# Hybrid diffusion step on one core: expert tiles renumbered, an add wait removed, adaLN sums in the eighth bank, last down product by halves

## The chip, the cores and the metric

One core of one Trainium2 chip. The metric is the device time of one execution in microseconds; of several runs the median is given. Everything is fp32.

## The reference, cut to what matters

Two trunk layers over 640 tokens (512 latent tokens and 128 context tokens, 1024 columns). Layer 0 mixes tokens by latent attention with 16 heads, layer 1 by neighbourhood attention. After each comes a mixture of experts: 16 experts in 4 groups of 4; a token picks one group and two experts in it. Each sub-layer has adaLN: shift, scale and gate rows computed from a conditioning vector by one product with a 1024 x 6144 matrix per layer.

```python
_, top_group = lax.top_k(group_score, TOPK_GROUPS)          # TOPK_GROUPS = 1
expert_mask = jnp.repeat(group_mask, EXPERTS_PER_GROUP, axis=-1) > 0
_, top_e = lax.top_k(jnp.where(expert_mask, biased, NEG_INF), TOP_K)   # TOP_K = 2
...
act = jax.nn.silu(jnp.einsum('td,edf->tef', t, w_gate)) * jnp.einsum('td,edf->tef', t, w_up)
act = act * gates.astype(act.dtype)[..., None]
return jnp.einsum('tef,efd->td', act, w_down).reshape(shp)
```

So the two experts of a token are always of one group, and two experts of different groups share no token.

## The kernel before, in words

Each engine has its own hand-written program, and semaphores join them. The program of one engine is strictly in order; a wait holds everything behind it on that engine. GpSimd (POOL) issues the gathers, the adds and the small stores; SyncE (SP) issues the weight loads; ScalarE (ACT) issues the loads and stores of x and h. The PSUM has eight banks of 512 columns.

**Attention of layer 0** (`mla_scores`, `mla_between`, `mla_pT`, `mla_pv`, L1036 to L1110). It runs over 40 steps w, five token tiles for each of eight head pairs. In step w TensorE makes the scores of the pair's two heads (L1065, L1068; banks 0 and 1, banks 2 and 3), then the transposes of step w-1 (banks 4 and 5, banks 6 and 7, at most 384 columns of each), then the product with V of step w-2. In one step of each pair an adaLN product (`ada(0, 4 + p)`, L809, 64 matmuls of 128 columns) stands between the two heads' scores. Its sums go to bank 3, columns 128 to 255 (`ada_bank`, `ada_out_at`), where the second head's scores come next. So TensorE waits for `m_cp` before them: VectorE's `ada_rows` has added the bias to the sums and written them to `modrow` (two operations for two of the eight). The adaLN product itself waits for `a_ex`, the exponentials of step w-1.

**Experts.** `f_stage` chooses experts and builds, on VectorE, tables of the tokens and gates of each tile of 128 slots; `tables_out` (L1955) copies them out of PSUM. Tile n holds the first 128 tokens of expert `EXPERT[n]`; slots without a token name a spare row behind the 640 real rows of the buffers in HBM. There are 15 static tiles (STAT), then the last expert's tile and the overflow tiles in a loop of 1 to 5 passes with two tiles each; `rtx` holds the count of passes and the experts. For a tile, POOL gathers the token rows, TensorE transposes them (`rows_T`), multiplies by gate and up weights (`gateup`, L1194), transposes the activations (`acts_T`), multiplies by the down weights (`down`, L1211), VectorE scales the result to `yb[n % 2]` (`y_out`), and POOL adds the rows to x in HBM with an accumulating indirect DMA (`add_rows`, L734; `add_static`). The tables are stored by expert number, and tiles of odd n use a second table (`odd_at`) with other spare rows.

Adds go through two semaphores `e_ys[l][0]` and `[1]`, 16 for each add, by the parity of the tile. Fourteen static adds leave both at 112. In a pass of the loop POOL issues a gather, waits in mid-pass until both counters are at 112 (128 in the second pass, and so on), issues a second gather, and then the two adds:

```python
for j in range(2):
    pool.wait_ge(e_yd[l], i * 2 + (STAT + j))
    pool.wait_ge(e_ys[l][1 - j], i * 16 + (112, 128)[j])
    pool.nop().then_inc(e_gate, 1)
    add_rows(last_token(j), j)
```

**The last tile** isn't added in HBM. Its down product goes to banks 1 and 2, VectorE writes y, and TensorE multiplies y by a 0/1 matrix (`at_token`) that puts its rows in token order (`last_part`, L1253), two products for each of five tiles of x. Meanwhile ACT waits for both add counters, in layer 0 also for the adaLN product `ada(1, 4)` (its weights lie in x's place), and loads the five tiles of x (L1628). VectorE's `x_sum` (L1698 on `resid`) adds the two. In layer 0 `ada(1, 4)` stands behind the last down product and ahead of `last_part`. After that come layer 1's norm, its transposes and the value projection (L934), or in layer 1 the final norm and the stores.

Of the kernel before, what the change touches and what calls it, by code (L numbers as in the profile page):

```python
# [57 lines left out]
EXPERT = (0, 4, 12, 8, 1, 5, 13, 9, 2, 6, 11, 7, 3, 10, 14)  # L58
ODD = slice(4, 11)
# [7 lines left out]
C_SPARE, C_SPARE_ODD = 257, 258  # L67
# [15 lines left out]
def constants():  # L83
    c = np.zeros((P, NCONST + NK), np.float32)
    p = np.arange(P)
    c[:, C_ID:C_ID + P] = np.eye(P)
    c[:, C_TRI:C_TRI + P] = p[:, None] < p[None, :]
    c[:, C_ONE:C_ONE + P] = 1.0

    qc, kc = p // ROWS, np.arange(LOCAL) // ROWS  # L90
    for n, (q0, k0) in enumerate(((0, 0), (48, 32))):
        q, k = q0 + qc[:, None], k0 + kc[None, :]
        start = np.clip(q - 8, 0, GRID_W - 16)
        at = C_MASK + n * LOCAL
# [8 lines left out]
    c[:, C_I16:C_I16 + E] = np.arange(E)  # L103
# [7 lines left out]
    c[:, C_SPARE] = TOK + p - 2048  # L111
    c[:, C_SPARE_ODD] = TOK + P + p - 2048
# [4 lines left out]
    k[:, K_BASE:K_BASE + E] = P * (E - 1) - np.arange(E) * P  # L117
    k[:, K_FIRST:K_FIRST + E] = E - np.arange(E)
    return c


def build(nc, a, o):

    with ExitStack() as ctx:
# [22 lines left out]
        rtx = sb("tiles", 32, 1, I32)  # L147
        wrt = sb("wrouter", KD * E)
        info = sb("info", 37)
# [76 lines left out]
        tok_at, gate_at, odd_at = info[:, 0:STAT], info[:, STAT:2 * STAT], info[:, 2 * STAT:2 * STAT + 7]  # L226
# [28 lines left out]
        hD, xD = ([nc.dram_tensor(f"{n}rows{l}", [TOK + spares * P, D], F32).ap() for l in range(DEPTH)] for n, spares in (("h", 1), ("x", 2)))  # L255
# [316 lines left out]
        def _(pool):  # L572
# [136 lines left out]
            for l in range(DEPTH):  # L709
# [21 lines left out]
                rows_of(tok_at[:, EXPERT[2]:EXPERT[2] + 1], 0)  # L731
# [8 lines left out]
                def add_static(n):  # L740

                    pool.wait_ge(e_yd[l], n + 1)
                    at, e = (odd_at, EXPERT[n] - ODD.start) if n % 2 else (tok_at, EXPERT[n])
                    add_rows(at[:, e:e + 1], n % 2)

                for n in range(3, STAT + 2):
# [3 lines left out]
                    rows_of(tok_at[:, EXPERT[n]:EXPERT[n] + 1] if n < STAT else last_token(n - STAT + 3), n % 2)  # L750
# [8 lines left out]
                with pool.Fori(0, trips) as i:  # L759
                    pool.wait_ge(e_tr[l], i * 2 + (STAT + 1))  # L760
# [24 lines left out]
        def _(pe):  # L785
# [262 lines left out]
            def mla_scores(w):  # L1048
# [6 lines left out]
                for par in range(2):  # L1055
# [5 lines left out]
                    if par and i == (1 if p else 0):  # L1061
                        pe.wait_ge(m_cp, 5 + p)
# [114 lines left out]
            def moe(l):  # L1177
# [25 lines left out]
                def down(b, w_in_, w_ready, tiles, free):  # L1203
# [8 lines left out]
                    ins.then_inc(e_dn[l], 1)  # L1212
# [21 lines left out]
                down(2, e_dw[l][0], trips * 16 + 16, trips * 2 + STAT, trips * 2 + (STAT - 1))  # L1234
                pe.wait_ge(e_dn[l], trips * 2 + STAT)

                pe.wait_ge(e_ta[l], trips * 2 + (STAT + 1))
                pe.wait_ge(e_td[l], trips * 2 + (STAT + 1))
                if l == 0:
                    ada(1, 4)  # L1240
                pe.wait_ge(e_yd[l], trips * 2 + STAT)
                pe.wait_ge(e_sel, l + 1)
                for t in range(4):
                    last_part(l, t)

            def last_part(l, t):
# [5 lines left out]
                for n in range(2):  # L1252
                    ins = pe.matmul(part_at(l, t)[:, n * 512:(n + 1) * 512], at_token[:, t * P:(t + 1) * P], yb[0][:, n * 512:(n + 1) * 512],  # L1253
# [14 lines left out]
            for u, (t, j) in enumerate(WIN):  # L1268
# [9 lines left out]
                if u == 0:  # L1278
                    last_part(0, 4)
# [97 lines left out]
            last_part(1, 4)  # L1377
# [3 lines left out]
        def _(act):  # L1381
# [153 lines left out]
            act.wait_ge(s_yz, 16 * 6)  # L1535
# [153 lines left out]
        def _(dve):  # L1689
# [85 lines left out]
            for b in (3, 6, 7):  # L1775
                link(dve.memset(bank(b, P, P if b == 3 else 0), 0.0))
# [103 lines left out]
            dve.wait_ge(s_yz, 16 * 6)  # L1880
# [74 lines left out]
            def tables_out(l):  # L1955

                dve.wait_ge(rr_cnt, 8 * l + 8)
                spare = const[:, C_SPARE:C_SPARE + 1]
# [3 lines left out]
                dve.tensor_scalar(odd_at.bitcast(U32), toks[:, ODD], const[:, C_SPARE_ODD:C_SPARE_ODD + 1], 2048.0, ALU.min, ALU.add)  # L1962
                for at in (last_tok[:, 2:15], last[:, 0]):
                    dve.tensor_scalar(at.bitcast(U32), toks[:, STAT - 1:], spare, 2048.0, ALU.min, ALU.add)
                dve.tensor_copy(last[:, 1], gates[:, STAT - 1:]).then_inc(e_tab[l], 1)

            def f_stage(l):
# [18 lines left out]
                tx, cmp_, at = rt[0:1, 1100:1132], rt[0:1, 1140:1284], rt[:, 1290:1310]  # L1986
# [79 lines left out]
                def first_places(t):  # L2066

                    dve.wait_ge(rr_cnt, 8 * l + max(t + 1, 2))
                    link(dve.scalar_tensor_tensor(out=u2[:, t], in0=rank[:, t, EXPERT[0]:EXPERT[1] + 1:EXPERT[1]], scalar=1.0, in1=M[:, t, EXPERT[0]:EXPERT[1] + 1:EXPERT[1]], op0=ALU.add, op1=ALU.mult))
# [61 lines left out]
                link(tt(pos, pos, const[:, C_E128:C_E128 + E].unsqueeze(1).to_broadcast([P, NT, E]), ALU.add))  # L2131
# [20 lines left out]
                link(dve.tensor_copy(tx[:, MAXT:MAXT + 5], const[0:1, C_FREE:C_FREE + 5]))  # L2152
                cm = cmp_.rearrange("p (x e) -> p x e", x=XTILES)
# [9 lines left out]
            def moe(l):  # L2163
# [38 lines left out]
                for n in range(STAT):  # L2202
                    if n == 2:
                        dve.wait_ge(e_tab[l], 1)
                    acts(gate_at[:, EXPERT[n]:EXPERT[n] + 1], n + 1, n or None)
# [4 lines left out]
                    if n < STAT - 1:  # L2210
                        gate_rows(tok_at[:, EXPERT[n]:EXPERT[n] + 1], 3 * n + 1, 3 * n + 2)
# [24 lines left out]
                y_out(trips * 2 + STAT, trips * 8 + (base + 3), 0, trips * 16 + 16 * 7)  # L2236
# [130 lines left out]
```

## Time and profile before

| | |
|---|---|
| runs, median of 3 | 1307.62 us (1306.54 to 1309.13) |
| the profiled execution's own time | 1304.3 us |
| its span | 1302.4 us, 19449 instructions |
| mean granted TensorE clock | 0.99 |
| TensorE matmuls busy | 1239.2 us, 95% |
| VectorE, ScalarE, GpSimd busy | 653.0, 341.8, 221.1 us |
| HBM traffic over the span | 203 GB/s |

In the timeline a row has its start in us from the span's start, the length in us of the row, the engine, the line, the operation, and what it writes and reads. "x64" says that 64 instructions of one kind are merged, and brackets give how long the engine sat idle before it and what released it. L1698 is a helper for VectorE's `tensor_tensor`, so the tile's name says which use it is. A row of windows has the stretch, then for each engine its busy time and instructions, the granted clock of TensorE as a part of full speed, the share of the DMA engines and GB/s. The span is slightly shorter than the time, and the profiled execution is 3.3 us below the median.

### The profile page before, as it was taken

The numbers are of one execution on the slowest core, as the hardware profiler recorded it, in microseconds if no ns is written. First come the engines' busy times: TensorE is split into PE (matmuls) and PEld (weight loads), VectorE is DVE, ScalarE is ACT, GpSimd is POOL, SyncE is SP. The second block draws the span as 40 slices with busy tenths as digits, with TensorE's granted clock in tenths as the row PEclk, the third lists the DMA queues.
The fourth block names the chain that finished last, engine by engine and source line by source line (L and its number), as shares of the span: only waits on it lengthen the run. The fifth ranks groups of instructions, "written<-read, shape, count | busy, mean of one in ns | idle before, by whom it ended". The sixth has DMA issues, their size and how long they took to land.

```text
span 1302.4 us, 19449 instructions
## 1 busy us (share of the span) xinstructions
PE 1239.2 (95%) x7503; PEld 713.0 (55%) x7503; DVE 653.0 (50%) x1612; ACT 341.8 (26%) x797; POOL 221.1 (17%) x298
## 2 busy tenths in 40 slices
PE   5899999999999999999989999999999998999995
PEld 3665466666645554444444455556884455444442
DVE  5221266556626664444455335432883666444446
ACT  4121255445403400000032000103891340000002
POOL 6220500010010012222120001040321001222220
PEclk8999999999999999999999999999999999999998
DMA  9612411131475459999971274542316336999966
GB/s 383 226 41 75 182 70 67 67 131 67 196 265 195 162 202 380 379 380 378 347 228 79 74 257 171 194 145 79 87 51 254 140 130 260 374 379 380 379 173 202
DMA packets 45450, 267.83 MB, mean 206 GB/s; under 512 B 6980, under 2 KB 13460, under 8 KB 31520
## 3 DMA queue, kind: packets, MB, share of 16 engines
q1 hardware_dynamic: 22672, 192.85, 37.9%
q0 software_dynamic: 16928, 52.77, 14.4%
q10 hardware_dynamic: 5760, 20.97, 4.2%
q8 instruction: 60, 0.98, 0.3%
q14 instruction: 30, 0.25, 0.1%
HBM read 230.19 MB, written 34.81 MB: 203 GB/s over the span
## 4 chain that ended last, share of the span: by engine, by line
PE 86%; DVE 6%; DMA 4%; issue 2%; ACT 1%; POOL 0%; ACTq 0%; POOLq 0%; DVEq 0%
PE PS L1194 15%; PE PS L934 13%; PE PS L1299 11%; PE PS L1148 10%; PE PS L1211 8%; PE PS L787 5%; PE PS L1065 5%; PE PS L793 4%; PE PS L1105 3%; PE PS L1357 2%; PE PS L809 2%; PE PS L1015 2%; PE PS L1320 1%; DVE big L1698 1%; PE PS L1068 1%
## 5 line engine op out<-in xcount | busy, mean ns | idle before, releaser
L1148 PE MATMUL PS<-weights,ht 128*128 128x512 f32 x320 | 142.4, 596 | 1.0 <-DVE ht L1698 1.0
L1299 PE MATMUL PS<-ht,weights 128*128 128x128 f32 (+1 forms) x512 | 140.2, 435 | 0.8 <-DMA weights<-in_qkv 0.8
L934 PE MATMUL PS<-weights,ht 128*128 128x336 f32 (+1 forms) x320 | 115.8, 520 | 1.6 <-ACT ht L1480 1.6
L1194 PE MATMUL PS<-big 128*128 128x512 f32 x256 | 113.1, 594 | 0.5 <-DVE big L2166 0.5
L1299 PEld LDWEIGHTS PS<-ht,weights 128*128 128x128 f32 x512 | 77.8, 191 | 63.4 <-issue 62.3
L787 PEld LDWEIGHTS PS<-const,big 128*128 128x128 f32 (+2 forms) x627 | 77.0, 144 | 57.1 <-issue 39.9
L787 PE MATMUL PS<-const,big 128*128 128x128 f32 (+2 forms) x627 | 92.1, 283 | 12.4 <-DVE big L1788 4.2
L1608 ACT ACTIVATE big<-PS 128x256 f32<-128x256 f32 x34 | 13.0, 383 | 337.1 <-PE PS L1194 337.1
L1148 PEld LDWEIGHTS PS<-weights,ht 128*128 128x128 f32 x320 | 59.0, 190 | 68.2 <-issue 68.2
L934 PEld LDWEIGHTS PS<-weights,ht 128*128 128x128 f32 x320 | 60.1, 190 | 52.2 <-issue 38.1
L1194 PE MATMUL PS<-weights,big 128*128 128x512 f32 x192 | 84.4, 592 | 0.0
L1698 DVE TENSOR_TENSOR big<-PS,big 128x512 f32<-128x512 f32 (+1 forms) x70 | 44.2, 672 | 69.8 <-PE PS L1211 69.8
L1194 PEld LDWEIGHTS PS<-big 128*128 128x128 f32 x256 | 47.4, 190 | 54.5 <-issue 54.5
L1942 DVE TENSOR_REDUCE stats<-PS 128x1 f32<-128x640 f32 (+1 forms) x80 | 56.7, 716 | 40.2 <-PE PS L1068 36.8
L611 POOL DMA_DIRECT2D modrows<-modrow x32 | 18.4, 583 | 342.6 <-DVE modrow L1698 263.3
L1698 DVE TENSOR_TENSOR big<-big,PS 128x256 f32<-128x256 f32 x34 | 14.3, 420 | 121.0 <-ACT big L1608 121.0
L1065 PE MATMUL PS<-big 96*128 96x512 f32 x128 | 69.2, 623 | 4.2 <-DVE modrow L1698 2.5
L1562 ACT ACTIVATE rows<-PS,stats 128x640 f32<-128x640 f32 (+1 forms) x80 | 56.4, 705 | 49.6 <-issue 32.5
L1211 PE MATMUL PS<-rows,big 128*128 128x512 f32 x144 | 65.1, 595 | 1.4 <-DVE big L2180 1.2
L1758 DVE SCALAR_TENSOR_TENSOR rows<-weights,condT,rows 128x512 f32<-128x512 f32 x98 | 65.5, 745 | 0.0
L734 POOL DMA_INDIRECT xrows<-big,info x28 | 44.4, 1586 | 117.4 <-DVE big L1698 117.4
L934 PE MATMUL PS<-weights,rows 128*128 128x384 f32 (+1 forms) x168 | 60.5, 518 | 0.2 <-ACT big L1519 0.2
(256 smaller groups left out, 1837.0 us busy)
## 6 DMA issues: line engine op xcount, KB each, us to landing
weights<-in_ada SPq DMA_DIRECT2D x22, 2048.0 KB, 8.9
big<-in_gu SPq DMA_DIRECT2D x16, 2048.0 KB, 20.1
weights<-in_gu SPq DMA_DIRECT2D x12, 2048.0 KB, 23.6
rows<-in_down SPq DMA_DIRECT2D x18, 1024.0 KB, 14.3
weights<-in_down SPq DMA_DIRECT2D x16, 1024.0 KB, 17.3
ht<-in_gu SPq DMA_DIRECT2D x6, 2048.0 KB, 23.0
weights<-in_qkv SPq DMA_DIRECT2D x6, 2048.0 KB, 8.6
weights<-in_wo SPq DMA_DIRECT2D x4, 2048.0 KB, 7.9
```

The lines of the kernel that those rows point to most:

```text
L787: return pe.transpose(dst, src, const[0:n, C_ID:C_ID + n])
L793: ins = pe.transpose(dst[:, at + 512 * r:at + 512 * r + 64], src[rows], const[rows, C_ID + 64 * r:C_ID + 64 * r + 64])
L934: ins = pe.matmul(bank(4 + u % 2, n), lhs(k), rhs(k), start=(k == 0), stop=(k == ks - 1))
L1065: pe.matmul(bank(2 * par), lhs, kTh[h % 4][0:QD, 0:512], start=True, stop=True)
L1148: ins = pe.matmul(bank(4 + j), OT[:, k, t * P:(t + 1) * P], w[j][:, k, :], start=(k == 0), stop=(k == KD - 1))
L1194: ins = pe.matmul(bank(0), gatT[:, k, :], w[:, k, :], start=(k == 0), stop=(k == KD - 1))
L1211: ins = pe.matmul(bank(1 + n), actT[:, k, :], w[:, k, n * 512:(n + 1) * 512], start=(k == 0), stop=(k == 1))
L1299: ins = pe.matmul(bank(bb, n1 - n0), w[:, k, m * P:(m + 1) * P], hT[:, k, n0:n1], start=(k == 0), stop=(k == KD - 1))
L1562: act.activation(dst, src, ACT.Exp, scale=sign, bias=st[:, 100 + at:101 + at], accum_out=st[:, 104 + at:105 + at]).then_inc(a_ex, 1)
L1698: return dve.tensor_tensor(dst, x, y, op)
L1758: dve.scalar_tensor_tensor(out=acc[c], in0=w[:, k, :], scalar=by, in1=acc[c], op0=ALU.mult, op1=ALU.add).then_inc(m_acc, 1)
L1942: dve.tensor_reduce(st[:, at:at + 1], bank(2 * par, n), AXX, ALU.max, negate=True).then_inc(a_mx, 1)
```

## The change

The parts of the diff:

1. `EXPERT` becomes 0, 4, 8, 12, 1, 5, 9, 13, 2, ... (groups in turn), and the tables are laid out by tile number instead of expert number. Even and odd tiles get their spare rows by a step of two over one table; `odd_at` goes. `hD` has two spare blocks as `xD` has. `tables_out` has eight operations, before it had six.
2. In the loop POOL waits for values that are read from a table (`C_LANDED`: 96, 128, 144, 160, 176) by a register load.
3. The adaLN sums of products 4 to 11 go to bank 7, columns 384 to 511. The wait for `m_cp` moves from before the second head's scores to before the second head's transposes, and the product waits for `a_pd`, VectorE's copy of the transposes of step w-2.
4. `ada(1, 4)` moves ahead of the last down product. That product signals after each half of its columns, VectorE writes y by halves and signals each, and `last_part` begins with the first.

```diff
-EXPERT = (0, 4, 12, 8, 1, 5, 13, 9, 2, 6, 11, 7, 3, 10, 14)
-ODD = slice(4, 11)
+EXPERT = [4 * (n % 4) + n // 4 for n in range(E)]
...
+    c[:, C_LANDED:C_LANDED + 5] = [96, 128, 144, 160, 176]
...
         def ada_bank(i):
-            return 2 if 12 <= i < 16 else 3 if 4 <= i < 12 else 6 + i % 2
+            return 2 if 12 <= i < 16 else 7 if 4 <= i < 12 else 6 + i % 2
         def ada_out_at(i):
-            return ada_bank(i) * 512 + (128 if 4 <= i < 12 else 0)
+            return ada_bank(i) * 512 + (384 if 4 <= i < 12 else 0)
...
             for l in range(DEPTH):
-                pool.dma_start(hD[l][TOK:, :], zero).then_inc(s_yz, 16)
-                for n in range(2):
-                    pool.dma_start(xD[l][TOK + n * P:TOK + (n + 1) * P, :], zero).then_inc(s_yz, 16)
+                for r in range(2):
+                    rows = slice(TOK + r * P, TOK + (r + 1) * P)
+                    pool.dma_start(hD[l][rows, :], zero).then_inc(s_yz, 16)
+                    pool.dma_start(xD[l][rows, :], zero).then_inc(s_yz, 16)
...
                 with pool.Fori(0, trips) as i:
+                    landed = pool.value_load(rtx[0:1, bass.ds(i + 32, 1)], min_val=96, max_val=176)
...
-                        pool.wait_ge(e_ys[l][1 - j], i * 16 + (112, 128)[j])
+                        pool.wait_ge(e_ys[l][1 - j], landed + (0, 16)[j])
...
                     if w:
-                        pe.wait_ge(a_ex, 2 * w)
+                        pe.wait_ge(a_pd, w - 1)
                     ada(0, 4 + p)
...
-                    if par and i == (1 if p else 0):
-                        pe.wait_ge(m_cp, 5 + p)
...
                     at = (4 + 2 * par) * 512
+                    if par and w % NT == 0:
+                        pe.wait_ge(m_cp, 5 + w // NT)
...
-                    ins.then_inc(e_dn[l], 1)
+                        if n or by_halves:
+                            ins.then_inc(e_dn[l], 1)
...
-                down(2, e_dw[l][0], trips * 16 + 16, trips * 2 + STAT, trips * 2 + (STAT - 1))
-                pe.wait_ge(e_dn[l], trips * 2 + STAT)
-
+                if l == 0:
+                    ada(1, 4)
+                down(2, e_dw[l][0], trips * 16 + 16, trips * 2 + STAT, trips * 2 + (STAT - 1), True)
...
-                if l == 0:
-                    ada(1, 4)
...
-                dve.tensor_scalar(tok_at.bitcast(U32), toks[:, 0:STAT], spare, 2048.0, ALU.min, ALU.add).then_inc(rr_info, 1)
+                for r in range(2):
+                    spare = const[:, C_SPARE + r:C_SPARE + r + 1]
+                    ins = dve.tensor_scalar(tok_at[:, r::2].bitcast(U32), toks[:, r:STAT:2], spare, 2048.0, ALU.min, ALU.add)
+                ins.then_inc(rr_info, 1)
...
-                y_out(trips * 2 + STAT, trips * 8 + (base + 3), 0, trips * 16 + 16 * 7)
+                dve.wait_ge(e_gr[l], trips * 8 + (base + 3))
+                dve.wait_ge(e_ys[l][0], trips * 16 + 16 * 7)
+                for n in range(2):
+                    half = slice(n * 512, (n + 1) * 512)
+                    dve.wait_ge(e_dn[l], trips * 2 + (STAT + n))
+                    tt(yb[0][:, half], bank(1 + n), grow[:, half], ALU.mult).then_inc(e_yd[l], 1)
```

## Rows read from the trace of the kernel before

**Rows 1.** The page, chain that ended last, shares of the span by engine.

```profile
PE 86%; DVE 6%; DMA 4%; issue 2%; ACT 1%; POOL 0%; ACTq 0%; POOLq 0%; DVEq 0%
```

**Rows 2.** Line L1065, TensorE's idle time before it: releaser, us, times.

```profile
  DVE modrow L1698: 2.5, 5
  DVE modrow L1771: 1.7, 2
```

**Rows 3.** Timeline, first attention: the first and the second head pair.

```profile
156.71 0.49 PE L1070 MATMUL PS<-big 96*128 96x128 f32 x2 [0.41 <-DVE modrow L1698]
...
178.32 0.96 DVE L1920 COPY rows<-PS 128x768 f32<-128x768 f32 x1 [0.45 <-PE PS L793]
...
180.88 1.93 PE L809 MATMUL PS<-weights,condT 128*2 128x128 f32 x64
...
182.87 0.29 DVE L1698 TENSOR_TENSOR modrow<-PS,ada_bias 128x128 f32<-128x128 f32 x1 [1.06 <-PE PS L809]
...
183.31 1.10 PE L1065 MATMUL PS<-big 96*128 96x512 f32 x2 [0.51 <-DVE modrow L1698]
```

**Rows 4.** Timeline, the table step of layer 0.

```profile
474.06 0.23 DVE L1960 TENSOR_SCALAR info<-PS,const 128x15 uint32<-128x15 f32 x1 [0.52 <-PE PS L903]
...
474.55 0.36 DVE L1964 TENSOR_SCALAR big<-PS,const 128x13 uint32<-128x13 f32 x2
...
474.90 0.41 DVE L1698 TENSOR_TENSOR big<-big,PS 128x256 f32<-128x256 f32 x1
...
476.58 7.11 PE L1194 MATMUL PS<-big 128*128 128x512 f32 x16 [0.25 <-DVE big L2166]
```

**Rows 5.** Timeline, GpSimd behind its zero stores, and ScalarE's first q store.

```profile
48.02 0.54 POOL L635 DMA_DIRECT2D big<-in_krope  x1
...
89.41 0.49 ACT L1519 ACTIVATE big<-PS 128x384 f32<-128x384 f32 x1
```

**Rows 6.** Timeline, end of layer 0's expert stage.

```profile
652.99 1.61 POOL L734 DMA_INDIRECT xrows<-big  x1 [0.30 <-issue]
...
653.43 1.29 DVE L1698 TENSOR_TENSOR big<-PS,big 128x512 f32<-128x512 f32 x2 [1.78 <-PE PS L1211]
...
660.87 3.70 PE L1211 MATMUL PS<-rows,big 128*128 128x512 f32 x8 [0.60 <-DVE big L2180]
660.92 1.58 POOL L734 DMA_INDIRECT xrows<-big  x1 [6.32 <-DMA xrows<-big]
...
664.91 1.93 PE L809 MATMUL PS<-resid,condT 128*2 128x128 f32 x64 [0.35 <-PE PS L1211]
666.77 7.13 PE L1253 MATMUL PS<-big 128*128 128x512 f32 x16
...
667.11 2.73 ACTq L1628 DMA_DIRECT2D resid<-xrows  x5
...
673.88 1.22 DVE L1698 TENSOR_TENSOR resid<-resid,PS 128x1024 f32<-128x1024 f32 x1 [1.91 <-DMA resid<-xrows]
```

**Rows 7.** Transfers into or out of xrows, 600 to 672; and a window's row.

```profile
DMA to landing us min/median/max: 3.5/7.4/13.5
...
676.00:677.00 1.00, 0.98 (x5) 0.98 (x6) 1.00 (x1) 0.58 (x3) 0.00 (x0) 0.56 0.98 307
```

**Rows 8.** Timeline, end of layer 1's expert stage.

```profile
1269.94 1.29 DVE L1698 TENSOR_TENSOR big<-PS,big 128x512 f32<-128x512 f32 x2 [1.78 <-PE PS L1211]
...
1275.20 1.58 POOL L734 DMA_INDIRECT xrows<-big  x1 [6.84 <-DMA xrows<-big]
...
1281.29 1.29 DVE L1698 TENSOR_TENSOR big<-PS,big 128x512 f32<-128x512 f32 x2 [0.21 <-PE PS L1211]
...
1282.83 8.82 PE L1253 MATMUL PS<-big 128*128 128x512 f32 x20 [1.76 <-DVE big L1698]
1284.92 1.22 DVE L1698 TENSOR_TENSOR resid<-resid,PS 128x1024 f32<-128x1024 f32 x1 [2.34 <-DMA resid<-xrows]
...
1286.54 1.22 DVE L1698 TENSOR_TENSOR resid<-resid,PS 128x1024 f32<-128x1024 f32 x1 [0.40 <-PE PS L1253]
```

More of the change, by code:

```diff
@@ L66 @@
 C_MASK = 384
-C_SPARE, C_SPARE_ODD = 257, 258
+C_SPARE = 257
+C_T128, C_LANDED = 260, 280
 C_COS, C_SIN = 896, 960
@@ L110, in constants @@
     c[:, C_SEL:C_SEL + E] = p[:, None] % 32 == np.arange(E)[None, :]
-    c[:, C_SPARE] = TOK + p - 2048
-    c[:, C_SPARE_ODD] = TOK + P + p - 2048
+    for r in range(2):
+        c[:, C_SPARE + r] = TOK + r * P + p - 2048
+    first_tile = np.argsort(EXPERT) * P
+    c[:, C_T128:C_T128 + E] = first_tile
+    c[:, C_LANDED:C_LANDED + 5] = [96, 128, 144, 160, 176]
     k = c[:, NCONST:]
@@ L146, in build @@
         rti = sb("slot_of", 6 * NT, P, U32)
-        rtx = sb("tiles", 32, 1, I32)
+        rtx = sb("tiles", 40, 1, I32)
         wrt = sb("wrouter", KD * E)
-        info = sb("info", 37)
+        info = sb("info", 30)
         rbias = rt[:, 1420:1436]
@@ L254, in build @@
         toepD = nc.dram_tensor("toeplitz", [H, 2 * ROWS, TLEN], F32).ap()
-        hD, xD = ([nc.dram_tensor(f"{n}rows{l}", [TOK + spares * P, D], F32).ap() for l in range(DEPTH)] for n, spares in (("h", 1), ("x", 2)))
+        hD, xD = ([nc.dram_tensor(f"{n}rows{l}", [TOK + 2 * P, D], F32).ap() for l in range(DEPTH)] for n in "hx")
         s_const, s_x, s_vec, s_par, s_ck = (sem(n) for n in ("const_in", "x_in", "vec_in", "gains_and_router_in", "mlacache_in"))
@@ L742, in add_static @@
                     pool.wait_ge(e_yd[l], n + 1)
-                    at, e = (odd_at, EXPERT[n] - ODD.start) if n % 2 else (tok_at, EXPERT[n])
-                    add_rows(at[:, e:e + 1], n % 2)
+                    add_rows(tok_at[:, n:n + 1], n % 2)
                 for n in range(3, STAT + 2):
@@ L749, in _ @@
                     pool.wait_ge(e_tr[l], n - 1)
-                    rows_of(tok_at[:, EXPERT[n]:EXPERT[n] + 1] if n < STAT else last_token(n - STAT + 3), n % 2)
+                    rows_of(tok_at[:, n:n + 1] if n < STAT else last_token(n - STAT + 3), n % 2)
                     if n >= 4:
@@ L1201, in acts_T, with down @@
                     ins.then_inc(e_at[l], 1)
-                def down(b, w_in_, w_ready, tiles, free):
+                def down(b, w_in_, w_ready, tiles, free, by_halves=False):
                     pe.wait_ge(w_in_, w_ready)
@@ L1252, in last_part @@
                 for n in range(2):
+                    if n and t == 0:
+                        second_half()
                     ins = pe.matmul(part_at(l, t)[:, n * 512:(n + 1) * 512], at_token[:, t * P:(t + 1) * P], yb[0][:, n * 512:(n + 1) * 512],
@@ L1376, in _ @@
             moe(1)
-            last_part(1, 4)
+            last_part(1, 4, None)
         @block.scalar
@@ L1534, in _ @@
             cq_out(3)
-            act.wait_ge(s_yz, 16 * 6)
+            act.wait_ge(s_yz, 16 * 8)
             q_store(0)
@@ L1772, in ada_rows @@
                 ins.then_inc(m_cp, 1)
-            for b in (3, 6, 7):
-                link(dve.memset(bank(b, P, P if b == 3 else 0), 0.0))
+            for b, at in ((6, 0), (7, 0), (7, 384)):
+                link(dve.memset(bank(b, P, at), 0.0))
             dve.wait_ge(s_vt, 1)
@@ L1879, in _ @@
             ckv_out(3)
-            dve.wait_ge(s_yz, 16 * 6)
+            dve.wait_ge(s_yz, 16 * 8)
             q_store(1)
@@ L1957, in tables_out @@
                 dve.wait_ge(rr_cnt, 8 * l + 8)
-                spare = const[:, C_SPARE:C_SPARE + 1]
                 toks, gates = bank(6, TILES), bank(6, TILES, TILES)
-                dve.tensor_scalar(tok_at.bitcast(U32), toks[:, 0:STAT], spare, 2048.0, ALU.min, ALU.add).then_inc(rr_info, 1)
+                for r in range(2):
+                    spare = const[:, C_SPARE + r:C_SPARE + r + 1]
+                    ins = dve.tensor_scalar(tok_at[:, r::2].bitcast(U32), toks[:, r:STAT:2], spare, 2048.0, ALU.min, ALU.add)
+                ins.then_inc(rr_info, 1)
                 link(dve.tensor_copy(gate_at, gates[:, 0:STAT]))
-                dve.tensor_scalar(odd_at.bitcast(U32), toks[:, ODD], const[:, C_SPARE_ODD:C_SPARE_ODD + 1], 2048.0, ALU.min, ALU.add)
                 for at in (last_tok[:, 2:15], last[:, 0]):
-                    dve.tensor_scalar(at.bitcast(U32), toks[:, STAT - 1:], spare, 2048.0, ALU.min, ALU.add)
+                    for r in range(2):
+                        spare = const[:, C_SPARE + r:C_SPARE + r + 1]
+                        dve.tensor_scalar(at[:, r::2].bitcast(U32), toks[:, STAT - 1 + r::2], spare, 2048.0, ALU.min, ALU.add)
                 dve.tensor_copy(last[:, 1], gates[:, STAT - 1:]).then_inc(e_tab[l], 1)
@@ L2068, in first_places @@
                     dve.wait_ge(rr_cnt, 8 * l + max(t + 1, 2))
-                    link(dve.scalar_tensor_tensor(out=u2[:, t], in0=rank[:, t, EXPERT[0]:EXPERT[1] + 1:EXPERT[1]], scalar=1.0, in1=M[:, t, EXPERT[0]:EXPERT[1] + 1:EXPERT[1]], op0=ALU.add, op1=ALU.mult))
+                    link(dve.scalar_tensor_tensor(out=u2[:, t], in0=rank[:, t, 0:EXPERT[1] + 1:EXPERT[1]], scalar=1.0, in1=M[:, t, 0:EXPERT[1] + 1:EXPERT[1]], op0=ALU.add, op1=ALU.mult))
                     dve.tensor_scalar(hot[0][:, t, :], rk[:, K_IOTA:K_IOTA + P], u2[:, t, 0:1], None, ALU.is_equal).then_inc(rr_hot, 1)
@@ L2130, in f_stage @@
                 link(tt(pos, pos, rank, ALU.add))
-                link(tt(pos, pos, const[:, C_E128:C_E128 + E].unsqueeze(1).to_broadcast([P, NT, E]), ALU.add))
+                link(tt(pos, pos, const[:, C_T128:C_T128 + E].unsqueeze(1).to_broadcast([P, NT, E]), ALU.add))
                 for c in range(2):
```

21 lines of the change are left out of this document (11 added, 10 removed).

## The prediction, made before the changed kernel ran

> **What bounds the kernel now.** I read the page first, then the chain that ended last, then the timeline where that chain leaves TensorE. The chain is 86% TensorE [rows 1], so an edit pays only where it takes something out of TensorE's line, or out of one of the short stretches where the chain leaves it. The change touches four such stretches: the eight head pairs of the first attention, the table step before each expert stage, the end of the first expert stage, and the end of the second.
>
> **First attention.** TensorE makes the two score products of a step, and in one step of each head pair it puts an adaLN product (L809, 64 matmuls, 1.93 us) between them. That product went to bank 3, which the second score product also writes, so TensorE then waited until VectorE had copied it out: 0.51 us in the pass shown [rows 3]. Over the stage these waits come to 2.5 us in five passes and 1.7 in two where VectorE makes two operations [rows 2], and 0.41 in the first pass [rows 3]: 4.6 in all. With the sums in bank 7 the second score product can follow at once. The wait moves ahead of the second head's transposes, which write bank 7. The score products between take over 1.1 us (their first part alone is 1.10), while the copy ended 0.35 us after the adaLN product (182.81 to 183.16), in the two longer passes some 0.3 later: both are over before the new wait. The adaLN product itself now waits for VectorE's copy of step w-2 out of banks 6 and 7. In the shown pass that copy ended at 179.28, 1.6 us before the product began [rows 3]: no cost. What follows on TensorE ran without a gap, so ScalarE and VectorE don't end it. I take 4.4 of the 4.6, since the gap left between two products isn't quite nothing, with 3.9 and 4.6 as ends.
>
> **Table step, twice.** It has 8 VectorE operations in place of 6: one more before the first gather is released, one more behind it. It is on the path: the second gate-up product waits for VectorE behind it [rows 4]. Three such operations took 474.55 to 474.90, 0.12 us each; the first, whose end something waits for, lasts 0.23. Two more cost 0.25 in a layer, 0.5 in both, with 0.4 and 0.9 as ends. The gather that is released some 0.15 later is wanted a whole gate-up product later, at 7 us: covered. The extra copy into the row of tile numbers falls into TensorE's table product, where VectorE sat idle 0.52 us [rows 4]: nothing; without that cover, 0.2.
>
> **Zero rows.** Two more stores of 512 KB from GpSimd, and everything behind them on its queue a microsecond later. The queue had issued all six and the krope load by 48.6; the first consumer, ScalarE's q store, ran at 89.41 [rows 5]. With 40 us of cover this is nothing, and nothing else of GpSimd's is due before.
>
> **End of the first expert stage.** Here the chain leaves TensorE. There is one pass of the dynamic loop in this trace, with the adds of tiles 14 and 15. GpSimd issued the first at 652.99, then sat 6.32 us until it had landed, and issued the second at 660.92, though its rows were ready at 654.72 (653.43 + 1.29) [rows 6]. ScalarE started the five loads of x at 667.11 when that landed, 6.2 us after its issue; VectorE's second x sum waited for them, 1.91 us, to 673.88 [rows 6]. Of the two waits that now use the new register only the second changes: both counters must reach 112 in mid-pass anyway, so the first never held anything. With it gone the second add follows the first. GpSimd has one more register load ahead of its gather; the trace times none, only the 0.30 before the first add in which the queue handles a wait, an increment and the issue; I take 0.5, with nothing and 1.0 as ends. That puts the first add at 653.5 and, after its 1.61 us and a gap of 0.3, the second at 655.4. How long it takes to land beside another is what the trace shows least: alone 6.2 us, the first one, beside a gather, until 660.9, up to 7.9; across the stage 3.5 to 13.5 with 7.4 as the median [rows 6, 7]. I take 7.4, nearest to the pair with a gather: landed at 662.8.
>
> Two other things must be ready then. ScalarE also waits for the adaLN product that reads its weights out of x. It moves ahead of the last down product: TensorE came free at 660.27 (0.60 before 660.87), so its 1.93 run to 662.2 and the down product starts at 662.25 instead of 660.87. The loads can go at 662.8, 4.3 us sooner. The token-order products (L1253, 7.13 us for four tiles) began at 666.77. Now the down product ends at 662.25 + 3.70 = 665.95; the first half of y, 0.65 us of VectorE after the down product's first half (664.1), is there by then, the second at 666.8, and the products start at 666.0 and go on without a gap, since the first takes 0.89 (7.13 / 8). Their second tile is done at 669.6, and that is as soon as the second x sum can run: 673.88 less 669.6 is 4.3, the same as the loads give. I take 3.8, since TensorE ends its four tiles only at 673.1 and must make the transposes after that; ends 1.0 (landing at 666) and 4.4. Further on, the projection, its weight loads (they wait for x loads and for TensorE itself) and the bias loads all shift along. The Trainium skill, "DMA: Bandwidth & Descriptors", section "Anatomy of one DMA", fits a GpSimd DMA as 2.0 us plus its bytes at 436 GB/s, an estimated 3.2 us for 512 KB; the lone add's row says 6.2 and decides. By the page the adaLN product would be the last to end and this term would be 4.4 in place of 3.8.
>
> **End of the second expert stage.** No adaLN product here. The second add was issued at 1275.20, and with the 6.2 us of the lone add x was loaded from about 1281.4; VectorE waited 2.34 us for it, to 1284.92; the second sum waited 0.40 for TensorE, to 1286.54 [rows 8]. Two edits meet. The second add goes 3.9 us sooner (its rows are ready at 1269.94 + 1.29), so x isn't last any more. And y comes by halves: VectorE had to make the selection matrix until 1281.1 and made y at 1281.29 to 1282.58; the products began at 1282.83 after a wait of 1.76 [rows 8]. Its first half can now run from 1281.1, so the products start at 1281.9, and while the first one runs (0.89 us) the second half comes. That is 0.9 us. From the second sum on the stage goes at VectorE's pace and keeps the shift. I take 0.9; ends 0.3 (x still late) and 1.2.
>
> **Renumbering** changes no count and no size: the same experts' weights, 15 static tiles, one pass. It lets neighbours be in flight, and costs nothing elsewhere.
>
> **Sum.** -4.4 + 0.5 - 3.8 - 0.9 = -8.6 us. The profiled execution took 1304.3 us, which becomes 1295.7; it lay 3.3 under the median of the runs, 1307.62, and the same sum against that is 1299.0.
>
> **Rivals.** (a) The two adds share the DMA engines and come out one behind the other: the second lands at 665 to 666, the first stage's end brings 1.5, and the sum is 6.3: 1301.3. For it: the first add took up to 7.9 beside a gather, the queue's median is 7.4 with weight loads beside, and GpSimd's adds read and write HBM [rows 6, 7]. Against it: at 655 to 663 the weight loads have mostly landed. The Trainium skill, same page, section "Issuing engines are not separate DMA queues", says that all DMAs run on the same 16 engines and interleave; so it speaks for this rival, and this trace has no two adds in flight to say by how much.
> (b) The attention's stalls come back elsewhere: VectorE's copy, the maxima and the next head's keys are late in turn, and 4.4 goes. The sum is 4.2: 1303.4. Against it, TensorE had no other gap in these passes, and the 1.28 us of score products cover a copy of 0.35.
> (c) The change doesn't do what it says: the loop's second wait still holds, because the add of tile 13 or the mid-pass wait on both counters is what ends last. Then only the attention and y by halves are left: 4.4 + 0.3 - 0.5 = 4.2, again 1303.4.
> (d) Slower. Both adds, the gather and, in the first layer, what is left of the loads slow each other so that the second add lands L us after its issue, and x is late by L - 11.7 in the first layer (655.4 against 667.1) and by L - 10.1 in the second (1271.3 against 1281.4). Against 4.4 saved and 0.5 paid, this passes +2.6 us from L = 14.2; with L = 15 it is 3.3 + 4.9 + 0.5 - 4.4 = +4.3, 1311.9. For it: 13.5 was seen for one transfer of this stage [rows 7]. Against it: that was beside weight loads.
> Something smaller goes either way. TensorE's granted clock averaged 0.56 from 676 to 677, so it was at 1.2 GHz for most of that, after the engine had been idle from 673.9 (666.77 + 7.13) [rows 6, 7]. In the new order that idle time is nearly gone, so the clock may stay at 2.4 GHz; VectorE's part is as long as before, so this is worth 0 to 0.5.
>
> **How the numbers follow.** A measurement of this kernel can tell some 0.2%, 2.6 us, from no change. Chances: my forecast 0.70, (a) 0.14, (b) and (c) 0.10 together, (d) 0.02; 0.04 for what I haven't seen, most of it within 0.2%. The forecast's own ends are -8.6 with 3.9, 4.4, 1.2, 0.3 and their opposites; all at once isn't likely, so 1297.2 to 1301.0. The range reaches through (a) to (b) and (c): 1296.6 to 1303.5. Faster by over 0.2% holds in all cases but (d), the unseen, and a small part of (b) and (c) where more is lost: 0.93; same 0.04, slower 0.03.
>
> **What would show it.** Right: no wait of L1065's products for modrow; the adaLN product and the second score product back to back; two GpSimd adds some 2 us apart in both layers; ScalarE's x loads near 662.8 on the old time scale; the first value projection 3.8 us sooner after the last gate-up; the last stage's products on y starting 0.9 sooner. Wrong: a new wait of the second head's transposes or of L809; x loads that still follow the second add by more than 9 us; a time over 1303.5.

## The result, and the profile after

The changed kernel took 1295.14 us (median of 6 runs, 1292.16 to 1300.87), the kernel before 1307.08 on the same chip: a ratio of 0.9912, with a 95% interval of 0.9889 to 0.9935. That is faster, as forecast, but by 11.5 us by the ratio (11.9 between the medians) where 8.6 were forecast, and 1.5 us below the range. Two more series of the changed kernel gave 0.9916 and 0.9922, so the best figure is about 10.9 us. The profiled execution took 1296.04 us, its span was 1294.3.

The chain that ended last is now 90% TensorE, from 86 [rows 1]; the page's row:

```profile
PE 90%; DVE 5%; ACT 2%; DMA 1%; issue 1%; ACTq 0%; DVEq 0%; SPq 0%
```

The first attention after, by the idle time ahead of TensorE's first score product (the answer to [rows 2]) and by the timeline of the second head pair (to [rows 3]; a row has start, length, engine, line, operation):

```profile
L1067 PE MATMUL PS<-big x128: 591/594/697, 158.0 to 346.9; 96*128 96x512 f32 x128
its engine sat idle before it (us, times) until:
  issue: 7.0, 30
  ACT rows L1567: 1.4, 8
```

```profile
179.25 0.96 DVE L1925 COPY rows<-PS 128x768 f32<-128x768 f32 x1 [0.45 <-PE PS L797]
...
181.81 1.93 PE L813 MATMUL PS<-weights,condT 128*2 128x128 f32 x64
...
183.67 1.13 PE L1067 MATMUL PS<-big 96*128 96x512 f32 x2
...
183.81 0.29 DVE L1703 TENSOR_TENSOR modrow<-PS,ada_bias 128x128 f32<-128x128 f32 x1 [1.06 <-PE PS L813]
```

No wait for modrow is left (the two idle times in the first fence are those of the weight loads, which run beside the products), and the score product starts as the adaLN product ends. The end of the first expert stage after, from its timeline (to [rows 6]):

```profile
650.58 1.61 POOL L738 DMA_INDIRECT xrows<-big  x1 [0.30 <-issue]
652.49 1.58 POOL L738 DMA_INDIRECT xrows<-big  x1 [0.30 <-issue]
```

```profile
656.80 1.93 PE L813 MATMUL PS<-resid,condT 128*2 128x128 f32 x64
...
658.66 3.70 PE L1215 MATMUL PS<-rows,big 128*128 128x512 f32 x8
...
660.24 2.43 ACTq L1633 DMA_DIRECT2D resid<-xrows  x5
...
662.20 6.36 PE L1258 MATMUL PS<-big 128*128 128x512 f32 x14
...
666.02 1.22 DVE L1703 TENSOR_TENSOR resid<-resid,PS 128x1024 f32<-128x1024 f32 x1 [0.49 <-PE PS L1258]
```

```profile
669.26 1.99 PE L791 MATMUL PS<-const,big 128*128 128x128 f32 x16
671.96 7.11 PE L938 MATMUL PS<-weights,ht 128*128 128x512 f32 x16 [0.71 <-ACT ht L1654]
```

The three fences are GpSimd's own rows, all engines' rows, and TensorE's own rows behind them. The adds go 1.9 us apart, the loads of x (L1633) 7.75 us after the second, and the second x sum waits for TensorE and no longer for a load. The end of the second stage (to [rows 8]):

```profile
1265.00 1.58 POOL L738 DMA_INDIRECT xrows<-big  x1 [3.76 <-DVE big L1703]
...
1273.04 2.27 ACTq L1633 DMA_DIRECT2D resid<-xrows  x5
...
1273.88 1.28 DVE L1703 TENSOR_TENSOR big<-PS,big 128x512 f32<-128x512 f32 x2
1274.82 8.82 PE L1258 MATMUL PS<-big 128*128 128x512 f32 x20 [0.86 <-DVE big L1703]
1276.81 1.22 DVE L1703 TENSOR_TENSOR resid<-resid,PS 128x1024 f32<-128x1024 f32 x1 [1.65 <-PE PS L1258]
...
1278.53 1.22 DVE L1703 TENSOR_TENSOR resid<-resid,PS 128x1024 f32<-128x1024 f32 x1 [0.50 <-PE PS L1258]
```

TensorE waits 0.86 where it waited 1.76, and no sum waits for x.

**Measuring by stretches.** The chain of waits gives each stage's start on TensorE. Of the changed kernel, start and length:

```profile
39.47 24.53 PE PS L938 x80
...
155.85 1.86 PE PS L813 x64
...
332.40 1.86 PE PS L813 x64
...
354.44 13.97 PE PS L1152 x32
...
617.91 3.44 PE PS L1215 x8
```

With the projection at 671.96, the first QK product of the second attention at 748.75, layer 1's second gate-up product at 1085.96 and the end at 1294.3, this gives five stretches (the third starts at the down product of 617.91). The same anchors in each kernel's chain, in us. Slow runs, one of the kernel before once more (1852.55 us) and one of the renumbering alone (1347.96), are left out of the ratios but stand in the medians.

| kernel | front, 39 to 156 | attention, 7 passes | stage 0's end to projection | on to QK | gate-up to the end | median | ratio |
|---|---|---|---|---|---|---|---|
| before | 114.70 | 180.96 | 58.50 | 76.26 | 209.32 | 1307.08 | 1 |
| before, again | 116.38 | 180.98 | 59.56 | 76.56 | 209.18 | 1307.23 | 0.9994 |
| renumbered alone | 114.69 | 181.01 | 58.64 | 76.11 | 210.21 | 1308.36 | 1.0015 |
| adds alone | 116.38 | 181.00 | 58.67 | 77.98 | 210.93 | 1305.89 | 0.9995 |
| bank 7 alone | 116.38 | 176.54 | 59.73 | 76.46 | 209.14 | 1301.59 | 0.9963 |
| **changed** | 116.38 | 176.55 | 54.05 | 76.79 | 208.34 | 1295.14 | 0.9912 |
| changed, again | 116.39 | 176.54 | 54.03 | 75.90 | 208.31 | 1295.81 | 0.9916 |
| changed, third | 116.37 | 176.56 | 54.38 | 76.43 | 208.24 | 1296.35 | 0.9922 |
| less bank 7 | 116.38 | 180.94 | 54.03 | 75.94 | 208.25 | 1299.77 | 0.9944 |
| less adds in flight | 116.38 | 176.54 | 59.64 | 76.65 | 209.11 | 1303.03 | 0.9979 |
| less adaLN move | 116.38 | 176.57 | 57.66 | 76.69 | 208.35 | 1300.64 | 0.9953 |
| less halves | 116.38 | 176.57 | 55.86 | 76.34 | 209.22 | 1300.51 | 0.9948 |
| less move and halves | 116.38 | 176.55 | 58.56 | 78.39 | 210.85 | 1302.74 | 0.9973 |
| changed, short tables | 116.38 | 176.56 | 54.04 | 76.26 | 208.28 | 1295.16 | 0.9911 |

### The profile page after: what moved, and what is told of

Its sections match the earlier page's. It is cut to its first block, busy times and chain, and to the rows that moved or that the text cites. A ratio compares the mean times of both kernels' runs of the same rounds, so it can differ in the third digit from the quotient of the medians.

```text
span 1294.3 us, 19464 instructions
## 1 busy us (share of the span) xinstructions
PE 1237.4 (96%) x7503; PEld 711.2 (55%) x7503; DVE 653.2 (50%) x1618; ACT 341.7 (26%) x797; POOL 222.6 (17%) x301
## 4 chain that ended last, share of the span: by engine, by line
PE 90%; DVE 5%; ACT 2%; DMA 1%; issue 1%; ACTq 0%; DVEq 0%; SPq 0%
PE PS L1198 17%; PE PS L938 13%; PE PS L1304 11%; PE PS L1152 11%; PE PS L1215 9%; PE PS L791 5%; PE PS L1067 5%; PE PS L797 4%; PE PS L1109 3%; PE PS L813 2%; PE PS L1362 2%; PE PS L1019 2%; PE PS L1325 2%; PE PS L1258 1%; DVE big L1703 1%
```

## Experiments

Three questions were open: whether each term of the sum is what its part gives, which of three edits gives the end of the first stage, and why the profiled executions differ by only 8.3 us (1304.3 to 1296.0) where the ratio says 11.5.

**Controls.** Both kernels once more, unchanged.

> The changed kernel once more, as a control. Two theories of why it gained 11.5 us where 8.6 were forecast. Theory T (the terms): attention is worth 5.0, the end of the first expert stage 4.5, that of the second 1.0, the table step costs 0.5, so the real change is 9.9 and the runs scatter around 0.9924 of before. Theory S (something not seen that shows only in runs outside the profiled one): the ratio stays at 0.991 or below, 11.5 us or more. In the profile: if the half-clock stretch at 41 to 44 us, in which the adaLN and latent products lost 1.7 us, belongs to the change, it is there again; if it is chance, TensorE shows 1.00 there and the span is some 1292.7 us.

> The kernel before once more, as a control for the scatter and for the profile. In the profile of before, the stretch from TensorE's first latent product to the first adaLN product of the attention took 114.70 us; in all five profiles of changed kernels so far it took 116.38, with TensorE granted half its clock at 40 to 44 us. Theory C (chance): this profile shows 116.4 as well, and the profile of before was simply lucky by 1.7 us, which is why profiled executions differ by 7 to 8 us and medians by 11. Theory E (the edit, by its two more zero stores in the front): 114.7 again. The time: 1306.7 within 1, ratio 1.000 within 0.001.

The changed kernel took 1295.81, 0.9916 [0.9898, 0.9935]: between theory T (0.9924) and theory S (0.991 or less), and the interval holds both. The kernel before took 1307.23, 0.9994 [0.9979, 1.0008]. The front decides the third question. Windows of the kernel before, of the first profile and then of the control (stretch, busy us of PE, PEld, DVE, ACT, POOL, granted clock, DMA share, GB/s):

```profile
40.00:42.00 2.00, 2.00 (x8) 1.34 (x8) 1.34 (x5) 0.01 (x1) 0.00 (x0) 1.00 0.97 347
42.00:44.00 2.00, 2.00 (x8) 1.33 (x7) 0.00 (x0) 0.00 (x0) 0.00 (x0) 1.00 0.84 322
```

```profile
40.00:42.00 2.00, 2.00 (x5) 1.31 (x4) 0.97 (x4) 0.00 (x0) 0.00 (x0) 0.51 1.03 362
42.00:44.00 2.00, 2.00 (x6) 1.15 (x6) 0.00 (x0) 0.00 (x0) 0.00 (x0) 0.64 0.83 305
```

The same program ran this stretch at 2.4 GHz once and mostly at 1.2 GHz the other time, and needed 1.68 us more (116.38 against 114.70). Twelve of the fourteen profiles have the longer front. One of the two short ones is the renumbering alone, which has the two more zero stores. So the profile of before was a lucky one; theory C holds, theory E doesn't, and 8.3 + 1.7 is 10.0. Another 0.7 is that the first stage's end was shorter in that profile than in the mean of the old ones, as is shown further down. The Trainium skill, "TensorE: Matmul & The Clock Gate", Part 1, says that one kernel shows different numbers of slow matmuls from run to run; these two profiles agree.

**The attention's part**, taken out of the changed kernel and put alone into the kernel before:

```diff
-            return 2 if 12 <= i < 16 else 7 if 4 <= i < 12 else 6 + i % 2
+            return 2 if 12 <= i < 16 else 3 if 4 <= i < 12 else 6 + i % 2
...
-                        pe.wait_ge(a_pd, w - 1)
+                        pe.wait_ge(a_ex, 2 * w)
...
+                    if par and i == (1 if p else 0):
+                        pe.wait_ge(m_cp, 5 + p)
...
-                    if par and w % NT == 0:
-                        pe.wait_ge(m_cp, 5 + w // NT)
```

> The changed kernel with the attention's part undone: adaLN sums of the first attention in bank 3 again, with the old waits. Theory T: 5.0 us slower than the changed kernel (ratio to before 0.9962), the second score product waits again 0.51 us in five passes and 0.85 in two for modrow. My prediction's term was 4.4. Rival (the stall would come back elsewhere): under 2 us slower.

> The kernel before with the attention's part alone: adaLN sums of the first attention in bank 7, with the new waits. If the part adds to the others (theory T), its profile shows the stretch from the first attention's first adaLN product to its last 4.4 us shorter (180.96 us in both profiles of before, 176.5 here) and the rest as in before; time 4.9 us less, ratio 0.9962. Rival (what was saved comes back in a later stage as a longer wait for weights): under 3 us less.

Without it 1299.77, 0.9944 [0.9927, 0.9960], 4.0 us more than the changed kernel measured beside it (5.0 expected); alone 1301.59, 0.9963 [0.9945, 0.9981], 4.8 less than before (4.9 expected). Without it the timeline has the wait again:

```profile
182.61 1.93 PE L813 MATMUL PS<-weights,condT 128*2 128x128 f32 x64
...
185.04 1.10 PE L1069 MATMUL PS<-big 96*128 96x512 f32 x2 [0.50 <-DVE modrow L1703]
```

The seven passes are 4.42 us shorter in every kernel with bank 7 and in none with bank 3. The last pass, from its adaLN product to the out projection, went from 22.58 (335.40 to 357.98) to 22.04 (332.40 to 354.44). That is 4.96 in all. Both medians keep most of it, so it adds to the other parts; whether some 1 us comes back later stays open (see "Left open").

**The first stage's end**, its three edits taken out one by one. The loop's old wait:

```diff
-                    landed = pool.value_load(rtx[0:1, bass.ds(i + 32, 1)], min_val=96, max_val=176)
...
-                        pool.wait_ge(e_ys[l][1 - j], landed + (0, 16)[j])
+                        pool.wait_ge(e_ys[l][1 - j], i * 16 + (112, 128)[j])
```

> The changed kernel with the loop's old wait (each add after the other of the same pass has landed; no register). Theory T: the wait was what held x's loads, so the second add goes 6 us after the first, x's loads in the first layer start at about 663.5 after last gate-up instead of at the adaLN product's end: x sums are late by some 3.5 us in the first layer, and by 0.5 to 1.5 in the second (y by halves still helps): 3.5 to 5 us slower, ratio to before 0.995 to 0.9965. Rival R (TensorE's order alone did it): under 1 us slower.

The old order and the whole y, first both, then each alone:

```diff
-                if l == 0:
-                    ada(1, 4)
-                down(2, e_dw[l][0], trips * 16 + 16, trips * 2 + STAT, trips * 2 + (STAT - 1), True)
+                down(2, e_dw[l][0], trips * 16 + 16, trips * 2 + STAT, trips * 2 + (STAT - 1))
                 pe.wait_ge(e_ta[l], trips * 2 + (STAT + 1))
                 pe.wait_ge(e_td[l], trips * 2 + (STAT + 1))
+                if l == 0:
+                    ada(1, 4)
...
-                for n in range(2):
-                    half = slice(n * 512, (n + 1) * 512)
-                    dve.wait_ge(e_dn[l], trips * 2 + (STAT + n))
-                    tt(yb[0][:, half], bank(1 + n), grow[:, half], ALU.mult).then_inc(e_yd[l], 1)
+                y_out(trips * 2 + STAT, trips * 8 + (base + 3), 0, trips * 16 + 16 * 7)
```

> The changed kernel with the old order at the stage's end: adaLN product behind the last down product, and y handed over whole. Theory T: with the adds in flight together x's loads still wait for the adaLN product, which now ends after the down product; TensorE's line has the same work, but it must wait 1.3 us for y in both layers less what the adaLN product covers (1.93, all of it in the first). First layer 0 to 1 us slower (the x loads go about 1.9 us after the down product's start at 656.8, so at about 662.5, and land at 664.5 to 666.5), second 0.9 slower: 1 to 2 us in all, ratio to before 0.993 to 0.9935. Rival R: the order is worth most of the 4.5 us: 4 us or more slower.

> The changed kernel with only the adaLN product put back behind the last down product; y still by halves. Theory O (x's loads hang on the adaLN product, and x's second sum hangs on the loads): loads at the adaLN product's end again, the first layer's tail as in the run with both undone, 4 to 4.5 us longer than in the changed kernel, second layer's as changed: time 4.3 us over the changed kernel, ratio to before about 0.995. Rival H (it is the whole y that cost there): 1 us or less.

> The changed kernel with y handed over whole; adaLN product ahead as in the change. TensorE's last down product ends at 663.95 in the changed kernel's second profile and its products on y began at 663.79. With the whole y they wait for both VectorE operations, 1.29 us, to 665.3: 1.4 us longer in the first layer if TensorE sets the pace there, 0.85 in the second: 2.3 us over the changed kernel, ratio to before 0.9935. If x's loads set the pace in the first layer instead: 0.85 only.

And the renumbering with the adds in flight, without the other three edits:

> The renumbering and the two adds in flight together, alone: adaLN sums in bank 3, old order and whole y at the stage's end. In the run that had this order with the sums in bank 7, the first layer took 58.56 us from the last down product seen to the value projection, the same as before (58.50 and 59.56). Theory O (adds and adaLN product each hold the loads of x, so one alone gives nothing): first layer 58.5 again, second 0.2 less, table step 0.5 more: ratio 1.000 within 0.001. Rival: the sum of parts, 3 us less, 0.9977.

The old wait cost 7.2 us against the control (1303.03; I expected 3.5 to 5), order and halves together 6.9 (1302.74; I expected 1 to 2, so the rival was right). Undoing the order alone cost 4.8 (1300.64; 4.3 expected). Undoing the halves alone cost 4.7 between the medians and 4.2 by the ratios (1300.51; 2.3 expected; 2.8 of it in the profile's stretches, the rest inside the two intervals). Adds alone gave 0.9995 [0.9981, 1.0009]: nothing that can be told, as theory O said. These don't sum: 7.2, 4.8 and 4.7 for an end that gives some 6 in all. The timelines say why. Of the adds alone:

```profile
657.82 1.58 POOL L738 DMA_INDIRECT xrows<-big  x1 [0.30 <-issue]
...
666.41 1.93 PE L813 MATMUL PS<-resid,condT 128*2 128x128 f32 x64
...
668.48 3.07 ACTq L1633 DMA_DIRECT2D resid<-xrows  x5
...
672.80 1.22 DVE L1703 TENSOR_TENSOR resid<-resid,PS 128x1024 f32<-128x1024 f32 x1 [4.10 <-DMA resid<-xrows]
...
675.80 1.22 DVE L1703 TENSOR_TENSOR resid<-resid,PS 128x1024 f32<-128x1024 f32 x1 [1.77 <-DMA resid<-xrows]
```

Of the changed kernel less the adds in flight:

```profile
657.50 2.26 POOL L738 DMA_INDIRECT xrows<-big  x1 [6.52 <-DMA xrows<-big]
...
664.31 2.41 ACTq L1632 DMA_DIRECT2D resid<-xrows  x5
...
671.73 4.07 PE L790 MATMUL PS<-const,big 128*128 128x128 f32 x16 [4.07 <-DVE big L2274]
```

The loads of x wait for the later of two things: in the first kernel the adaLN product, which ends at 668.34, 0.14 before them, and in the second the add. Taking one away leaves the other. In the kernel before they were close in the profile of the prediction: the adaLN product ended at 666.84 (664.91 + 1.93), 0.27 before the loads [rows 6]. In the other three old ends (before again, renumbering alone, bank 7 alone) it ended 2.4 to 2.8 us before them. With the adds alone the loads then take 4.3 us to the first sum and 7.3 to the second (668.48 to 672.80 and 675.80). Without the adds in flight TensorE runs out of work for 4.07 us, and what follows at once runs at the lower clock: 16 transposes take 4.07 us too, where they take 1.99 in the changed kernel (3.80 in the first profile of before). A window of the kernel without the adds in flight, and one of the changed kernel in the same stretch:

```profile
674.00:676.00 2.00, 2.00 (x9) 1.94 (x10) 2.00 (x5) 2.00 (x5) 1.62 (x4) 0.50 0.96 410
```

```profile
674.00:676.00 2.00, 2.00 (x6) 0.86 (x5) 1.46 (x5) 1.92 (x5) 1.99 (x4) 1.00 0.99 422
```

In all five profiles with this end whole (the changed kernel three times, less bank 7, short tables) this stretch stays at 2.4 GHz. It falls in both profiles of before, with the renumbering, the adds or bank 7 alone, and wherever the adds in flight or the order is undone; with only the halves undone it doesn't.

**The renumbering alone**, with its spare tables and zero stores, and **a shorter table step**:

> Only the renumbering with its two-row spare tables and its two more zero stores; adaLN sums in bank 3, old loop wait, old order and whole y at the stage's end. By the prediction's terms: table step +0.25 in each layer, all else 0: 0.5 us slower than before, ratio 1.0004. Theory E (front's 1.7 us belong to this part): 2.2 us slower, 1.0017. A third (neighbours written in order change the adds' landing): some tenths in either layer's tail.

> The changed kernel with the table step cut from 8 VectorE operations to 5: each pair of operations over even and odd tiles becomes one, against a table of spare rows in the constants. If the table step's term is right (an operation is 0.12 us there, on the path): 0.24 to 0.36 us less from the table to the second gate-up product in each layer, 0.6 in all: too little for the median to tell from the changed kernel, but the profile's stretch from the last out projection to that gate-up product must be shorter by it. Rival: nothing, because the gather behind it sets that product.

```diff
-                for r in range(2):
-                    spare = const[:, C_SPARE + r:C_SPARE + r + 1]
-                    ins = dve.tensor_scalar(tok_at[:, r::2].bitcast(U32), toks[:, r:STAT:2], spare, 2048.0, ALU.min, ALU.add)
-                ins.then_inc(rr_info, 1)
+                spare = const[:, C_SPTAB:C_SPTAB + TILES]
+                dve.scalar_tensor_tensor(out=tok_at.bitcast(U32), in0=toks[:, 0:STAT], scalar=2048.0, in1=spare[:, 0:STAT], op0=ALU.add, op1=ALU.min).then_inc(rr_info, 1)
```

(and likewise the two pairs behind it; the table of spare rows, TOK + 128 (n % 2) + p for tile n and row p, is in the constants.) The step shows in the idle time before TensorE's next two transposes in layer 0. It was 1.05 us before; with the renumbering alone, and then with the short tables, it is:

```profile
476.46 0.44 PE L790 MATMUL PS<-const,big 128*128 128x128 f32 x2 [1.30 <-DVE big L2183]
```

```profile
473.53 0.44 PE L793 MATMUL PS<-const,big 128*128 128x128 f32 x2 [0.73 <-DVE big L2182]
```

So 0.25 us paid for two operations, as in the sum, and 0.57 won back by three fewer. In layer 1 the renumbering alone has 1.64 and the short tables 0.87. The renumbering's ratio was 1.0015 [1.0004, 1.0027], 2.0 us slower against the 0.5 expected, which is at the interval's edge; without its one run of 1347.96 its median is 1307.86, 0.9 over the 1307.01 of the kernel before beside it. Its profiled span is 2.0 us over the first of before as well: 0.3 ahead of the first latent product, 0.25 and 0.59 in the two table steps, and 0.9 in the second stage's end, where GpSimd waited 7.57 us for the first add against 6.84 [rows 8]. Whether the numbering or chance makes that wait longer can't be told from one profile. The short tables gave 1295.16, 0.9911 [0.9890, 0.9932], beside the control:

> The changed kernel a third time, as the control beside the shorter table step: 1295.5 within 1, ratio 0.991 to 0.992. In its profile the first expert stage's end is 54.0 us and without a stretch at half clock, as in both so far; the fall at 40 to 44 us is there.

which took 1296.35, 0.9922 [0.9900, 0.9944]. The two intervals overlap, so only the profile speaks for the short tables, with 1.0 us less in the two gaps.

## Why the prediction was right in its mechanisms and short in its sum

- **First attention.** Right in where and why; the term of 4.4 should have been 4.96. I took something off the 4.6 of waits "since the gap left between two products isn't quite nothing". It was the other way round: a product that waits also loses the overlap with the one before it, so a pass got 0.55 shorter for a wait of 0.51 [rows 3]. Even my upper end, 4.6, was too low. Rival (b) fell, as far as the medians can tell.
- **Table step.** 0.5, as forecast. The register's load, priced at 0.5 us, cost nothing that shows: from GpSimd's add to the gather behind the load in layer 1 it is 2.50 us in before (1254.26 to 1256.76) and 2.51 with the load (1260.55 to 1263.06, adds alone). The first add came at 650.58, on the old scale 654.0 (the stage began 3.41 sooner), against 653.5 forecast: the gather landed later (a wait of 9.13 against 8.48) and a copy took 1.15 us against 0.58.
- **End of the first stage.** The step that failed, by size: the term of 3.8 measured 5.1. The second add's landing (7.75 us against 7.4) as the later of the two things the loads wait for, the start of L1258 (662.20, which is 665.6 on the old scale, against 666.0) and the second sum (669.4 against 669.6) came as forecast, and rival (a) fell. But from the resulting 4.3 I took 0.5 off, because TensorE ends its tiles late, and set the clock's worth at 0 to 0.5. In the profile the projection came 4.45 sooner: TensorE was late for the transposes, but ran them in 1.99 us where the old kernel needed 3.80. And the old end varies with how late the loads of x land. From the mid-stage down product to QK it took 134.76, 136.12, 134.75 and 136.19 us in the four old ends, 135.5 in the mean (the second x sum ran 52.6, 53.3, 52.4 and 53.4 us after that down product), and 130.84, 129.93, 130.81, 129.97 and 130.30 in the five new ones, 130.4: 5.1 us, where I had 3.8. The one profile that I read had one of the shortest. I also took the second add's landing as what started its loads (667.11); the adaLN product had ended only 0.27 before them, so there the two were nearly level.
- **End of the second stage.** 0.9 forecast, 0.98 between the two first profiles; 1.2 between means (209.46 over the four old, 208.28 over the five new), but the renumbering's 210.21 alone raises that mean, and without it the difference is 0.93. The size was right.
- **Sum.** 4.96 - 0.5 + 5.1 + 0.9 = 10.5 against 10.9 measured. The stretch under "Left open" takes 0.4 off that sum in the mean of the changed kernel's three profiles, and the intervals are wider than either gap, so the agreement is no proof of the last half microsecond. The Trainium skill, "DMA: Bandwidth & Descriptors", section "Anatomy of one DMA", has the fit that gave an estimated 3.2 us for the add; by it the first stage's term was 4.4, nearer to 4.45, but the 7.75 us from the add's issue to the loads refutes the landing that it rests on.
- **Range.** Its low end came from one execution's rows. The terms for waits could each come out larger than the wait seen, and none of my ends allowed for that. 0.5 of the miss is the base as well: 1307.62 was a median of three runs, with six it is 1307.08, and later series gave 1306.5 to 1307.2.

Left open: around 450 us, in the routing of layer 0, the stretch from the last adaLN product to the second gate-up product has two lengths in kernels with bank 7, about 1.45 us apart (140.77 and 142.23 in two profiles of the same changed kernel), by how long the clock stays at its lower level. Six of nine profiles with bank 7 have the longer one, none of five with bank 3 (141.08 to 141.42, with the last pass still 0.54 longer). If that isn't chance, the attention's part gives back about 1 us there, which its median of 4.8 doesn't exclude.

## What to carry to other kernels

When a transfer waits for two things, price the edit on each with the other in place. Here the adds in flight alone were worth nothing, and the moved adaLN product with y by halves nothing at this end without them (136.29 us from the down product to QK, against 135.5). Adds and move together gave 3.3 us (132.20), and with the halves 5.1. Where TensorE itself waits, the length of the wait was slightly less than what its removal gave (0.51 against 0.55 in an attention pass), and with an idle stretch went the slow stretch behind it (16 transposes in 1.99 us for 3.80). And a profile is one draw: a sum that is made against one execution takes over its luck, here 1.68 us in the front and 0.7 in the first stage's end, so read a second profile of the same kernel first.

## Not expected of the hardware

With TensorE busy for all of 2.00 us in a window, its granted clock was still 0.51 at 40 to 42 us in one execution and 1.00 in another of the same program, worth 1.68 us. Of two GpSimd adds of 512 KB issued 1.9 us apart, the second took 7.2 to 8.0 us from its issue to the loads of x that waited for it (layer 0, six profiles, 7.6 in the mean), against 6.2 to 7.3 for the later one where each waits for the other (five profiles, 6.7 in the mean): some 0.9 us for company, where rival (a) had set 10. In layer 1, issued 5.4 us behind the first, it took 6.1 to 8.0. GpSimd's copies of 128 x 13 took 0.19 to 1.29 us in the same place from one execution to another; why wasn't tried:

```profile
647.16 1.15 POOL L774 COPY big<-big 128x13 f32<-128x13 f32 x1 [0.17 <-POOL big L771]
```

Not tried: the adds in flight without the renumbering, since neighbouring tiles would then share a spare row.
